# Feed-forward of a hybrid-attention kernel: which operand of the gate and up products is stationary

## The reference, cut to what matters

```python
def rms_norm(x, g):
    y = xf * lax.rsqrt(jnp.mean(xf * xf, axis=-1, keepdims=True) + EPS)
    return (y * g).astype(x.dtype)

def swiglu(x, w_gate, w_up, w_down):
    return (jax.nn.silu(x @ w_gate) * (x @ w_up)) @ w_down

x = x + 0.5 * swiglu(rms_norm(x, norm_ffn1[l]), w_gate[l], w_up[l], w_down[l])
```

## Time and profile before

| | |
|---|---|
| median of 3 runs | 1839.82 us |
| the profiled execution, its own time | 1841.48 us |
| its span, first to last instruction | 1839.8 us |
| mean granted TensorE clock | 0.998 |
| busy: PE, PE weight loads | 1794.3 us (98%), 1459.0 us (79%) |
| busy: DVE, ACT, POOL | 1122.3 us (61%), 936.7 us (51%), 195.0 us (11%) |
| moved from HBM | 313.94 MB, 171 GB/s |
| matmuls | 8740, as many weight loads |

### The profile page before, as it was taken

One profiled execution on the slowest core, in us unless ns is written; L12 is line 12 of the kernel. 1 busy time (PEld: TensorE's weight loads), 2 busy tenths in 40 slices (PEclk: granted clock), 3 DMA queues, 4 the chain that ended last, 5 costly groups with the idle time before them and its releaser, 6 DMA issues.

```text
span 1839.8 us, 23640 instructions
## 1 busy us (share of the span) xinstructions
PE 1794.3 (98%) x8740; PEld 1459.0 (79%) x8740; DVE 1122.3 (61%) x1649; ACT 936.7 (51%) x1266; POOL 195.0 (11%) x226
## 2 busy tenths in 40 slices
PE   7999999999999999999999999999999999999999
PEld 6888887788888888877888876778888777788887
DVE  5555676655555555777555489765554688765553
ACT  5444475544454444666444476655444656745441
POOL 0000020000000000200000095100001383000000
PEclk9999999999999999999999999999999999999999
DMA  8556462465556564543555464445555544345551
GB/s 254 184 191 222 139 184 93 151 197 191 196 157 189 190 218 143 181 130 123 186 192 196 160 206 142 156 138 175 187 194 190 203 145 155 130 147 181 186 207 64
DMA packets 221017, 316.21 MB, mean 172 GB/s; under 512 B 14056, under 2 KB 162176, under 8 KB 220672
## 3 DMA queue, kind: packets, MB, share of 16 engines
q1 hardware_dynamic: 220928, 315.03, 52.5%
HBM read 313.94 MB, written 1.05 MB: 171 GB/s over the span
## 4 chain that ended last, share of the span: by engine, by line
PE 81%; DVE 8%; issue 3%; ACT 3%; DVEq 2%; POOL 1%; DMA 1%; SPq 1%; POOLq 0%; ACTq 0%
PE ps L1829 25%; PE ps L1831 24%; PE ps L1830 24%; DVE w_lo L1145 2%; PE ps L1938 2%; ACT w_hi L679 1%; PE ps L1839 1%; PE ps L2034 1%; PE ps L2022 1%; PE ps L2010 1%; PE ps L1973 1%; DVE score L1604 1%; DVE att L1362 1%; DVEq L1607 1%; PE ps L2314 1%
## 5 line engine op out<-in xcount | busy, mean ns | idle before, releaser
L1145 DVE TENSOR_TENSOR w_lo<-raw,w_hi 128x2048 fp32r<-128x2048 f32 (+1 forms) x297 | 671.1, 2281 | 242.3 <-ACT w_hi L679 241.0
L1829 PE MATMUL ps<-w_hi,aT_hi 128*128 128x512 f32 (+2 forms) x1728 | 690.3, 399 | 12.9 <-DVE w_lo L1298 4.8
L1831 PE MATMUL ps<-w_hi,aT_lo 128*128 128x512 f32 (+2 forms) x1728 | 671.3, 388 | 0.0
L1830 PE MATMUL ps<-w_lo,aT_hi 128*128 128x512 f32 (+2 forms) x1728 | 669.4, 387 | 0.0
L679 ACT ACTIVATE w_hi<-raw 128x2048 fp32r<-128x2048 f32 (+1 forms) x297 | 554.7, 1899 | 182.4 <-PE ps L1831 178.8
L1829 PEld LDWEIGHTS ps<-w_hi,aT_hi 128*128 128x128 f32 x1728 | 325.8, 189 | 90.4 <-issue 15.2
L1831 PEld LDWEIGHTS ps<-w_hi,aT_lo 128*128 128x128 f32 x1728 | 325.4, 188 | 68.4
L1830 PEld LDWEIGHTS ps<-w_lo,aT_hi 128*128 128x128 f32 x1728 | 326.4, 189 | 59.6
L729 ACT ACTIVATE att<-ps,rstd 128x256 f32<-128x256 f32 x132 | 55.6, 472 | 377.9 <-PE ps L1831 377.8
L1219 DVE SCALAR_TENSOR_TENSOR att<-ps,rstd,att 128x256 f32<-128x256 f32 x132 | 57.8, 479 | 287.3 <-ACT att L729 287.3
L1829 PE MATMUL ps<-w_hi,gT_hi 128*128 128x512 f32 x528 | 207.1, 392 | 0.0
(11 more groups left out here) (265 smaller groups left out, 1398.0 us busy)
## 6 DMA issues: line engine op xcount, KB each, us to landing
raw<-in_w_in SPq DMA_DIRECT2D x120, 512.0 KB, 4.5
raw<-in_w_ffn_gate SPq DMA_DIRECT2D x88, 512.0 KB, 4.1
raw<-in_w_ffn_up SPq DMA_DIRECT2D x88, 512.0 KB, 5.1
raw<-in_w_ffn_down SPq DMA_DIRECT2D x88, 512.0 KB, 4.4
raw<-in_w_ffn_in SPq DMA_DIRECT2D x88, 512.0 KB, 4.9
raw<-in_w_ffn_out SPq DMA_DIRECT2D x44, 512.0 KB, 4.6
raw<-in_w_out SPq DMA_DIRECT2D x32, 512.0 KB, 4.7
raw<-in_w_ck SPq DMA_DIRECT2D x8, 512.0 KB, 4.2
```

What stands on the lines that cost most here:

```text
L1145: V.tensor_tensor(o, a, h, ALU.subtract).then_inc(units_split, 1)
L1829: M(o, ah, wh, start=start, stop=False)
L1830: M(o, ah, wl, start=False, stop=False)
L1831: return M(o, al, wh, start=False, stop=stop)
```

## The change

Ten of the eleven tiles of each feed-forward (all but the first) get other operands: a block of 128 weight columns is stationary and all 256 tokens of `aT` are moving. The result has the hidden columns in the partitions, gate in one bank (two blocks of 256 columns) and up in the next, and needs no turn. Since the token now lies in the free axis, the factor `rstd` can't be a scalar per partition any more: after the first tile DVE multiplies the identity with `rstd` into a diagonal, PE multiplies a block of ones with it (which yields the row of all 256 factors in each partition, bank 5), and DVE copies that row twice into `rstd_row`. In a turned tile DVE multiplies the gate with the row (signal `gate_scaled`), ACT applies Silu in place on 512 columns, and DVE multiplies the up half into `gg` without any factor; the up side's factor moves to the residual (`sum_scale`, `rstd` times 0.5 or 1). `keep` reads `gg` in SBUF instead of a PSUM bank, and comes before the tile's own work in ACT's and DVE's order. The first tile keeps its old operands and its turn, behind tile 1; its `gg` no longer has the factor either.

```diff
+        ones = sb("ones", [P, P])
+        sum_scale = sb("sum_scale", [P, 2])
+        rstd_diag = att[:, 2048:2304]
+        rstd_row = rot_end[:, :]
...
+            nc.gpsimd.memset(ones[:, :], 1.0)
...
 # ACT
+                def tile(t, pt, it=0):
+                    for j in range(2):
+                        split(st, pt + 2 + j, it)
                     b = pt // 2 - p0 // 2
+                    keep(t - 1, b + 1)
+                    act.wait_ge(gate_scaled, F * (FT - 1) + t)
+                    s = sil[:, b % 2].rearrange("p i n -> p (i n)")
+                    nc.scalar.activation(s, s, ACT.Silu).then_inc(silu_done, 1)
...
                 def keep(t, b):
...
+                    act.wait_ge(g_ready, F * FT + t + 1)
+                    nc.scalar.activation(gT_hi[:, bass.ds(t * 2, 2), :], gg[:, b % 2], ACT.Copy).then_inc(gT_hi_done, 1)
...
 # DVE
+                def tile(t, pt, it=0):
+                    for j in range(2):
+                        split(st, pt + 2 + j, it)
                     b = pt // 2 - p0 // 2
+                    keep(t - 1, b + 1)
+                    dve.wait_ge(units_used, st.used(pt + 1, it))
+                    s = sil[:, b % 2].rearrange("p i n -> p (i n)")
+                    V.tensor_tensor(s, ps[:, 2 * (b % 2), :], rstd_row, ALU.mult).then_inc(gate_scaled, 1)
                     dve.wait_ge(silu_done, F * FT + t + 1)
+                    V.tensor_tensor(gg[:, b % 2].rearrange("p i n -> p (i n)"), ps[:, 2 * (b % 2) + 1, :], s, ALU.mult)\
+                        .then_inc(g_ready, 1)
+
+                def first_tile():
+                    norm(N)
                     for i in range(2):
+                        o = V.tensor_scalar(rstd_diag[:, P * i:P * i + P], ident[:, :], rstd[:, i:i + 1], None, ALU.mult)
+                    o.then_inc(diag_ready, 1)
+                    V.tensor_scalar(sum_scale[:, :], rstd[:, 0:2], scale, None, ALU.mult)
+                    dve.wait_ge(row_T, F + 1)
+                    V.tensor_copy(rstd_row[:, 0:SEQ], ps[:, 5, 0:SEQ])
+                    V.tensor_copy(rstd_row[:, SEQ:2 * SEQ], ps[:, 5, 0:SEQ])
+                    dve.wait_ge(silu_done, F * FT + 1)
+                    for i in range(2):
+                        o = V.tensor_tensor(gg[:, 0, i], ps[:, i, 256:512], sil[:, 0, i], ALU.mult)
                     o.then_inc(g_ready, 1)
...
 # PE
+                def turned_tile(t, pt, it=0):
                     b = pt // 2 - p0 // 2
+                    for j in range(2):
+                        p = pt + j
+                        split_ready(st, p, it)
+                        if j == 0 and not (isinstance(t, int) and t < 2):
+                            pe.wait_ge(g_ready, F * FT + t - 1)
+                        for n in range(4):
+                            o = ps[:, 2 * (b % 2) + n // 2, SEQ * (n % 2):SEQ * (n % 2) + SEQ]
+                            for c in range(4):
+                                k, w = 4 * j + c, 512 * c + P * n
+                                wh, wl = w_hi[:, st.slot(p), w:w + P], w_lo[:, st.slot(p), w:w + P]
+                                M(o, wh, aT_hi[:, k, :], start=k == 0 and n % 2 == 0, stop=False, skip_group_check=True)
+                                M(o, wh, aT_lo[:, k, :], start=False, stop=False, skip_group_check=True)
+                                r = M(o, wl, aT_hi[:, k, :], start=False, stop=k == KC - 1, skip_group_check=True)
+                        r.then_inc(units_used, 1)
...
+                full_k(st, S, p0, 0, (0, 1), 512, second_half(x, x_ready, X, banks))
+                pe.wait_ge(diag_ready, F + 1)
+                M(ps[:, 5, 0:SEQ], ones[:, :], rstd_diag, start=True, stop=True).then_inc(row_T, 1)
+                turned_tile(1, p0 + 2)
+                pe.wait_ge(g_ready, F * FT + 1)
+                for c in range(2):
+                    for i in range(2):
+                        o = nc.tensor.transpose(ps[:, 4, SEQ * c + P * i:SEQ * c + P * i + P],
+                                                gg[:, 0, i, P * c:P * c + P], ident[:, :])
+                o.then_inc(g_T, 1)
+                turned_tile(2, p0 + 4)
                 with pe.Fori(0, 4) as it:
-                    both(it * 2 + 3, p0 + 6, it)
-                    both(it * 2 + 4, p0 + 8, it)
-
+                    turned_tile(it * 2 + 3, p0 + 6, it)
+                    turned_tile(it * 2 + 4, p0 + 8, it)
+
+                pe.wait_ge(g_ready, F * FT + FT - 1)
...
                     wide(st, p0 + U_UP + u, u, gT_hi, gT_lo, 2 * u, order=(1, 0) if u == 0 else (0, 1),
-                         between=(lambda: turn(FT - 1, FT - 1)) if u == 0 else None)
+                         between=(lambda: pe.wait_ge(g_ready, F * FT + FT)) if u == 0 else None)
```

More of the change, by code:

```diff
@@ L250, in build @@
         stage_ready = sem("stage_ready")
+        diag_ready = sem("diag_ready")
+        row_T = sem("row_T")
+        gate_scaled = sem("gate_scaled")
         silu_done = sem("silu_done")
@@ L728, in tile, with first_keep @@
+                def first_tile():
+                    root(N)
+                    act.wait_ge(units_used, st.used(p0 + 1))
                     for i in range(2):
-                        o = nc.scalar.activation(sil[:, b % 2, i], ps[:, 2 * (b % 2) + i, 0:256], ACT.Silu,
-                                                 scale=rstd[:, i:i + 1])
+                        o = nc.scalar.activation(sil[:, 0, i], ps[:, i, 0:256], ACT.Silu, scale=rstd[:, i:i + 1])
                     o.then_inc(silu_done, 1)
-                    if not first:
-                        keep(t - 1, b + 1)
+                def first_keep():
+                    act.wait_ge(g_T, F + 1)
+                    nc.scalar.activation(gT_hi[:, 0:2, :], ps[:, 4, :].rearrange("p (c n) -> p c n", c=2), ACT.Copy)\
+                        .then_inc(gT_hi_done, 1)
@@ L735, in keep @@
                 def keep(t, b):
[L737 to L742, removed]
+                    if isinstance(t, int) and t == 0:
+                        first_keep()
+                        return
@@ L743, in ffn @@
+                    act.wait_ge(g_ready, F * FT + t + 1)
+                    nc.scalar.activation(gT_hi[:, bass.ds(t * 2, 2), :], gg[:, b % 2], ACT.Copy).then_inc(gT_hi_done, 1)
+                first_tile()
+                for t in range(1, 3):
+                    tile(t, p0 + 2 * t)
                 with act.Fori(0, 4) as it:
@@ L1221, in tile @@
                     o.then_inc(g_ready, 1)
[L1222 to L1223 removed]
+                    V.drain()
                 def keep(t, b):
                     dve.wait_ge(gT_hi_done, F * FT + t + 1)
[L1227 to L1229 removed]
@@ L1230, in ffn @@
-                for t in range(3):
-                    tile(t, p0 + 2 * t, first=(t == 0))
+                    if isinstance(t, int) and t == 0:
+                        g = ps[:, 4, :].rearrange("p (c n) -> p c n", c=2)
+                    else:
+                        g = gg[:, b % 2]
+                    V.tensor_tensor(gT_lo[:, bass.ds(t * 2, 2), :], g, gT_hi[:, bass.ds(t * 2, 2), :].bitcast(F32),
+                                    ALU.subtract).then_inc(gT_ready, 1)
+                first_tile()
@@ L1241, in ffn @@
                     split(*args)
-                residual(st, R, p0 + U_UP + U_DOWN - 1, scale, S, gain, final=final)
+                residual(st, R, p0 + U_UP + U_DOWN - 1, None, S, gain, final=final)
             def tj(T, k, dst, bank, sign=1.0):
@@ L1931, in turn @@
[L1931 to L1946, removed]
-                for t in range(3):
-                    both(t, p0 + 2 * t, 0, t)
+                    for j in range(2):
[12 more added lines that the diff above has]
+                        r.then_inc(units_used, 1)
```

25 lines of the change are left out of this document (4 added, 21 removed).

## The result

| | before | after |
|---|---|---|
| median of 5 runs each | 1839.82 us | 1853.16 us |
| lowest to highest | 1838.51 to 1845.45 | 1852.77 to 1854.98 |
| ratio, 95% interval | | 1.0068 [1.0052, 1.0084] |
| profiled execution, its own time | 1841.48 us | 1852.77 us |
| its span | 1839.8 us | 1851.1 us |

The kernel became slower by 13.3 us, or 0.7%. That lies inside the range of the forecast, 1816 to 1858, which was wide, but not where it put most: its sum was +0.2 us and "no change" the likeliest, and what came is the number of the rival "the stationary load is the limit", 1852 to 1863.

What follows compares the result with a forecast made beforehand. PE alone was taken to bound the feed-forward tiles. Products +24.5, removed turns -26.7 and the scale row +2.4 summed to +0.2 us: 1841.7 us against the profiled execution, 1840.0 against the median, range 1816 to 1858.

Steps and rivals of the forecast that it cites:

- the stationary load is the limit: Gate and up products: overlapping weight loads slow long streams to 0.120 to 0.122 us a start, 1852 to 1863; chance 0.22.
- PE alone sets this loop: Feed-forward tiles, 11.367 us each: ACT waits for PE, so only changes to PE's own stream change the time.
- the products term: Ten tiles per feed-forward: 96 products of 256 columns at 0.118 us replace 48 of 512, +24.5 us in all.
- Its own upper bound: Products of 256 columns: at worst the extra per start equals that at 512, 0.014 us, giving 0.121 us.
- The two faster rivals: Products of 256 columns take 0.1138 us (about 1815.5 us, chance 0.20) or 0.115 us (1823 us, chance 0.12).
- The rule weighed beside them: Products cost N / 2.4 + 2.5 ns by the Trainium skill, which would make the sum -17 us.
- the first rival: Products of 256 columns: columns count, starts hardly do, 0.1138 us each, -24.3 us, about 1815.5; chance 0.20.
- the second's: Products of 256 columns: a start costs only a small constant, 0.115 us each, -17 us, 1823; chance 0.12.
- the turns: Transposes removed from ten of eleven tiles per feed-forward, 0.445 us of PE each, 60 in all: -26.7 us.
- the row product: One product of ones and a diagonal per feed-forward, giving the scales as a row: 0.41 us, six times, +2.4 us.
- the work beside PE, costed at nothing: DVE and ACT work behind each tile: a chain of 2.1 us, hidden with 2.7 us of slack on DVE.
- the way back of PE's loop: Loop return of PE must fetch code, 1.7 us showing at each of 18 returns: +31 us, 1871; chance 0.08.

Runs made afterwards that it cites:

- run 6: Changed kernel with the loaded weight blocks at uneven offsets, 30 to 120 floats ahead of their place: 1842.54 us, 10.6 below the changed kernel.
- run 1: Changed kernel with 240 instead of 256 token columns per product in nine of the ten turned tiles: 1812.53 us, ratio 0.9847 to the kernel before.
- run 5: Kernel before without the turns of ten tiles, gated values going untransposed into the down phase: 1812.8 us, ratio 0.9853.
- run 12: Changed kernel with two products joined into one of 512 columns, plus activations and all behind them shifted by 30: 1858.59 us, ratio 1.0087 to the kernel before.
- run 8: Changed kernel, all products whole, with high and low activations shifted by 30 and 60 floats: 1859.94 us, ratio 1.0098 to the kernel before.
- run 9: Kernel before with high and low activations shifted by 30 and 60 floats: 1861.33 us, ratio 1.0102.
- run 10: Changed kernel with high and low activations shifted by 32 and 64 floats: 1860.86 us, ratio 1.0097 to the kernel before.

## Why the prediction was right and wrong

**Right: what bounds it.** "PE alone sets this loop" held in every run; in each, the tile is as long as its starts.

**Wrong: the size of the products term.** The range held, the likeliest value did not. The forecast took 0.118 us for a product of 256 columns and got +24.5 us; it is 0.120. By the same formula 60 x (11.52 - 10.92) = +36.0, 11.5 more, and the sum of +0.2 becomes +11.7, where the spans differ by 1851.1 - 1839.8 = 11.3. The 0.118 was read rightly from its rows. Long runs have it too where the loaded blocks stand unevenly (run 6), and short ones from even places have it for their first products. What failed is the transfer to runs that are both long and from even places. The prediction had named both differences, the offsets in one rival and the short runs in another, but held the offsets to speak for a faster stream only. Its own upper bound, "what a start costs beyond its columns is the same as at 512", was the better rule: 0.2267 - 0.2133 and 0.120 - 0.1067 are both 13.3 ns.

**The slower rival that came true** had the number (0.120), the point of decision, and the picture of a stream that settles in a long run; its reason does not hold as it stands. It laid the limit on overlapping loads; these recur at 0.112 where 240 columns move (run 1). Why 256 columns from even places settle at 0.120 stays open. The two faster rivals fell. Less company of ACT and DVE, on which the first of them counted, made no difference that shows: uneven blocks take 0.118 in the busy compression and in a quiet tile (run 6).

The rule weighed beside them fell too, the Trainium skill's N / 2.4 + 2.5 ns ("TensorE: Matmul & The Clock Gate", "Back-to-back issue gap"). That section gives it for isolated products and says that it leaves out the loads; the prediction took it for a stream with a load in front of each product, and called it the first rival where its -17 us are the second's. The runs here show 13.3 ns beyond the columns at 256 and 512 and 11.7 at 248.

**Nearly right: the turns**, -26.7 forecast, -27.1 by the medians (run 5), but -29.2 by the tiles: one without its turn takes 10.88 us, not 10.92, so the turn cost 11.367 - 10.88 = 0.487 us, above the 0.445 that the forecast had also made its upper bound. It had put 0.04 us of the turn on the products; in the sum that cancels.

**Right: the row product**, 0.43 us for 0.41, without a wait for its diagonal. Timeline of DVE after the change:

```profile
26.08 0.48 DVE L1245 TENSOR_SCALAR att<-ident,rstd 128x128 f32<-128x128 f32 x2
...
62.60 0.69 DVE L1237 TENSOR_TENSOR att<-ps,rot_end 128x512 f32<-128x512 f32 x1 [3.23 <-PE ps L1975]
63.99 0.69 DVE L1239 TENSOR_TENSOR att<-ps,att 128x512 f32<-128x512 f32 x1 [0.70 <-ACT att L736]
```

The diagonal is done at 26.56 and PE comes to it at 26.99: 0.43 us of cover, 0.4 had been worked out.

**Right: the work beside PE, costed at nothing.** The chain DVE, ACT, DVE runs from 62.60 to 64.68, 2.08 us (2.1 forecast), and DVE then still waits 3.23 us for PE in a tile (2.7 of slack forecast).

**Did not happen: the way back of PE's loop.** Every tile of the loop takes 11.52 us, whether a return lies in it or not. The queue that fetches instructions moved 63 packets in the whole execution, 55 before, so not one more for each of the 18 returns. The 31 us of that rival are zero.

## What to carry to other kernels

Where TensorE sets the time, count starts and not only columns: here a start with its load costs 11 to 13 ns beyond its columns, so exchanging the operands doubled the starts and cost 38 us for the 29 of transposes that it saved, while joining two products that share a loaded block won 25 back. Every product here has a load of its own, so whether the price belongs to the start or to the load is not shown. Read the price of a changed stream from one of the same length, width and place in memory; where the nearest rows differ in one of these, give the bound that they don't reach a good share of the chance, all the more where one nanosecond is 6 us.

## What was not expected of the hardware

- **A stream of 256-column products from even places settles** at 0.1200 us a start, after five to ten products at 0.118 behind other work. 248 columns take 0.1150, 240 take 0.1120, 192 take 0.1117: between 248 and 240 a floor is reached, and the last eight columns of 256 cost 5.0 ns.
- **The place in SBUF changes TensorE's rate.** Loaded weight blocks at uneven columns: 0.1200 becomes 0.1181. Activations shifted by 30 and 60 or by 32 and 64 numbers: 512-wide products that load them go from 0.2267 to 0.2333 in one stretch, those that load `gT` stay at 0.2267. With everything shifted by 30 (run 12) those that load `gT` go to 0.2333. All four kernels with a shift (runs 8, 9, 10 and 12) were slower than the same kernel without, by 5 to 27 us going by their ratios; for runs 8 and 10 the start distances show it, the intervals of the times overlap. The cause was not found, and no other shifts were tried.
